# Adding the experts' results into the residual in DRAM by indirect DMAs, instead of on VectorE

## What is computed

```python
x = x + hierarchical_moe(rms_norm(x, g), ...)

def hierarchical_moe(h, ...):            # cut to what matters
    expert, gate = two_best_experts_of_the_best_group(h)      # 2 of 32 for each token
    for e in range(32):                                       # weights: 1024x512, 1024x512, 512x1024
        y_e = (silu(h[tokens of e] @ w_gate[e]) * (h[tokens of e] @ w_up[e])) @ w_down[e]
    return for each token: gate_1 * y_(first expert) + gate_2 * y_(second expert)
```

## Time and profile before

| | us |
|---|---|
| median of three executions | 1812.06 |
| the profiled execution | 1808.48 |
| its span, from the first to the last instruction | 1806.6 |
| TensorE matmuls busy | 1689.5 (94%) |
| VectorE busy | 661.4 (37%) |
| ScalarE busy | 449.3 (25%) |
| GpSimd busy | 170.4 (9%) |

### The profile page before, as it was taken

One profiled execution on the slowest core, in us unless ns is written; L12 is line 12 of the kernel. 1 busy time (PEld: TensorE's weight loads), 2 busy tenths in 40 slices (PEclk: granted clock), 3 DMA queues, 4 the chain that ended last, 5 costly groups with the idle time before them and its releaser, 6 DMA issues.

```text
span 1806.6 us, 21815 instructions
## 1 busy us (share of the span) xinstructions
PE 1689.5 (94%) x8694; PEld 869.9 (48%) x8694; DVE 661.4 (37%) x1266; ACT 449.3 (25%) x807; POOL 170.4 (9%) x172
## 2 busy tenths in 40 slices
PE   7999999799999999999699998999799999999983
PEld 3455454445445555455345558965433333333331
DVE  3279341432122212122468946542522212221223
ACT  2233671233221112111448403332000000000002
POOL 0000000011111111110000013100111111111100
PEclk9999999799999999999899999999799999999997
DMA  9265531399999999999560181054799999999994
GB/s 363 102 238 183 199 129 47 127 397 402 401 401 405 409 403 399 402 413 413 194 246 1 21 128 48 1 208 194 270 396 398 405 408 407 404 420 409 418 417 183
DMA packets 94220, 515.26 MB, mean 285 GB/s; under 512 B 22429, under 2 KB 28157, under 8 KB 69544
## 3 DMA queue, kind: packets, MB, share of 16 engines
q1 hardware_dynamic: 82920, 496.46, 70.7%
q0 software_dynamic: 11200, 17.39, 2.9%
HBM read 506.09 MB, written 27.05 MB: 295 GB/s over the span
## 4 chain that ended last, share of the span: by engine, by line
PE 76%; DMA 13%; DVE 6%; ACT 2%; SPq 2%; issue 1%; DVEq 0%; POOLq 0%
PE bank L863 23%; PE bank L879 11%; PE bank L464 10%; PE bank L456 8%; DMA ring<-in_w_up 6%; DMA ring<-in_w_down 4%; PE bank L850 3%; PE bank L820 3%; PE bank L1232 3%; PE bank L890 2%; PE bank L522 2%; PE bank L687 2%; PE bank L449 1%; DVE arena L2608 1%; PE bank L729 1%
## 5 line engine op out<-in xcount | busy, mean ns | idle before, releaser
L865 PE MATMUL bank<-ring,arena 128*64 128x512 f32 x928 | 421.9, 609 | 0.0
L863 PE MATMUL bank<-ring,arena 128*64 128x512 f32 x752 | 339.4, 605 | 7.3 <-DMA ring<-in_w_up 4.7
L2507 DVE TENSOR_TENSOR arena<-arena,bank 64x512 f32<-64x512 f32 x70 | 48.3, 690 | 561.9 <-ACT arena L1801 561.9
L879 PE MATMUL bank<-ring,arena 128*64 128x512 f32 x544 | 248.0, 598 | 2.3 <-DMA ring<-in_w_down 2.3
L881 PE MATMUL bank<-ring,arena 128*64 128x512 f32 x544 | 247.9, 598 | 0.0
L456 PE MATMUL bank<-arena,ring 128*128 128x512 f32 x560 | 246.3, 596 | 0.0
L863 PEld LDWEIGHTS bank<-ring,arena 128*64 128x64 f32 x752 | 100.7, 139 | 207.0 <-issue 200.9
L863 PE MATMUL bank<-arena 128*64 128x512 f32 x368 | 167.4, 609 | 9.4 <-DMA ring<-in_w_up 5.7
L1801 ACT ACTIVATE arena<-bank 64x512 f32<-64x512 f32 x70 | 41.2, 589 | 512.7 <-PE bank L865 512.7
L1440 POOL DMA_INDIRECT arena<-xnd,smalli x70 | 67.7, 968 | 1058.3 <-PE bank L850 535.9
L456 PEld LDWEIGHTS bank<-arena,ring 128*128 128x128 f32 x560 | 105.8, 191 | 128.1 <-issue 128.1
(11 more groups left out here) (441 smaller groups left out, 1989.7 us busy)
## 6 DMA issues: line engine op xcount, KB each, us to landing
ring<-in_w_down SPq DMA_DIRECT2D x62, 2048.0 KB, 23.2
ring<-in_w_up SPq DMA_DIRECT2D x54, 2048.0 KB, 21.2
ring<-in_w_gate SPq DMA_DIRECT2D x45, 2048.0 KB, 13.4
arena<-in_w_gate SPq DMA_DIRECT2D x19, 2048.0 KB, 25.1
ring<-in_w_mod SPq DMA_DIRECT2D x12, 2048.0 KB, 15.2
ring<-in_w_in SPq DMA_DIRECT2D x10, 2048.0 KB, 17.3
arena<-in_w_up SPq DMA_DIRECT2D x10, 2048.0 KB, 29.3
ring<-in_w_out SPq DMA_DIRECT2D x4, 2048.0 KB, 11.2
```

Of the source, the lines that this page charges most:

```text
L863: pe.matmul(GU[0:CAP, :], x, wg_[:, c, :], start=(c == 0), stop=(c == KD - 1), skip_group_check=True)
L865: mm = pe.matmul(GU[CAP:2 * CAP, :], x, wu_[:, c, :], start=(c == 0), stop=(c == KD - 1), skip_group_check=True)
L879: pe.matmul(Y[0:CAP, :], x, wd_[:, c, 0:512], start=(c == 0), stop=(c == 3), skip_group_check=True)
```

## The change

`yd` and `x2d` are gone. At the start of each stage SyncE stores x_tok in `xd[m]`, 512 rows in DRAM. The scatter adds (`compute_op=ALU.add`) to the rows of `xd[m]`, where a token's first and second expert meet; so each scatter waits until the one before it has landed, and the first one until x_tok is stored. In MoE 0 the share is multiplied by ScalarE on the way out of PSUM. At the end four tile loads bring the sum into x_tok, and VectorE adds nothing. The order on SyncE after MoE 0 is changed: five of the six weights come first, then the tile loads, then the sixth. The tables of rows and tokens are now one, and the shares are made in both stages.

```diff
+            def load_x(m):
+                for q in range(2):
+                    sp.wait_ge(S(f"stored{q}"), 16 * ((BASE[m] + NB[m]) // 2))
+                sp.wait_ge(S("added"), m + 1)
                 for t in range(TT):
+                    sp.dma_start(x_tok[:, t, :], xd[m][P * t:P * t + P, :]).then_inc(S(f"y_in{t}"), 16)
...
                 sp.wait_ge(S("gathered1"), 16 * (BASE[m] // 2 + 1))
+                sp.wait_ge(V.free, V.at(f"outB1{TORDER[-1]}" if m else f"outA1{TT - 1}"))
+                sp.dma_start(xd[m].rearrange("(t p) d -> p t d", p=P), x_tok).then_inc(S("x_out"), 16)
...
             experts(0)
 
-            for q in range(2):
-                sp.wait_ge(S(f"stored{q}"), 16 * (NB[0] // 2))
-            sp.wait_ge(S("yd_done"), 1)
-            load_y(0, yg2)
-            sp.wait_ge(S("x2_ready"), 2)
-            load(U_K)
-            sp.wait_ge(S("x2_ready"), TT)
-            sp.dma_start(x2d.rearrange("(t p) d -> p t d", p=P), x_tok).then_inc(S("x2_out"), 16)
-            for u in range(U_Q, U_DFT + 1):
+            for u in range(U_K, U_DFT):
                 load(u)
+            load_x(0)
+            load(U_DFT)
...
                 def scatter(n):
                     u = n % 2
                     pool.wait_ge(S("y_taken"), n0 + n + 1)
+                    if n:
+                        all_stored(n - 1)
+                    else:
+                        pool.wait_ge(S("x_out"), 16 * (m + 1))
                     pool.indirect_dma_start(
                         out=halves, out_offset=bass.IndirectOffsetOnAxis(ap=homes_any[:, n:n + 1], axis=0),
-                        in_=ys[u], in_offset=None, bounds_check=4 * T - 1, oob_is_err=False)\
+                        in_=ys[u], in_offset=None, bounds_check=2 * T - 1, oob_is_err=False, compute_op=ALU.add)\
                         .then_inc(S(f"stored{u}"), 16)
+
+                def all_stored(n):
+                    pool.wait_ge(S(f"stored{n % 2}"), 16 * ((n0 + n) // 2 + 1))
...
-                    A(ys[q], Y[:, :], ACT.Copy).then_inc(S("y_taken"), 1)
+                    if n == 0:
+                        act.wait_ge(CV.free, CV.at("shares0"))
+                    A(ys[q], Y[:, :], ACT.Copy, scale=share[0][:, n:n + 1]).then_inc(S("y_taken"), 1)
...
-                    act.wait_ge(S("x2_ready"), t + 1)
+                    act.wait_ge(S(f"y_in{t}"), 16 + 16)
                     chain(A(junk, x_tok[:, t, :], ACT.Square, accum_out=ssq[:, t:t + 1]))
...
-                    dve.wait_ge(S(f"y_in{t}"), 16 + 32)
-                    o = x_tok[:, t, :]
-                    chain(STT(o, yg2[t][0], w12[:, t:t + 1], o, ALU.mult, ALU.add))
-                    STT(o, yg2[t][1], w12[:, TT + t:TT + t + 1], o, ALU.mult, ALU.add).then_inc(S("x2_ready"), 1)
...
-                dve.wait_ge(S(f"y_in{t}"), 16 + 64)
-                o = x_tok[:, t, :]
-                chain(TTo(o, o, yg[t][0], ALU.add))
-                TTo(o, o, yg[t][1], ALU.add).then_inc(S("x4_ready"), 1)
```

More of the change, by code:

```diff
@@ L123, in build @@
         xnd = [dram(f"xnd{m}", (T, D)) for m in range(2)]
-        yd = [dram(f"yd{m}", (2 * T, D)) for m in range(2)]
-        x2d = dram("x2d", (T, D))
+        xd = [dram(f"xd{m}", (T, D)) for m in range(2)]
         diag = dram("diag", (2, 16, 8, 16, 16))
@@ L907, in spots @@
                         for r in (0, CAP):
-                            mm = pe.matmul(b[r:r + CAP, 0:NBLK[m] + 1], in_place[:, c, :], at_block[m][:, c, :],
+                            mm = pe.matmul(b[r:r + CAP, 0:NBLK[m]], in_place[:, c, :], share_at[m][:, c, :],
                                            start=(c == 0), stop=(c == 2 * TT - 1), skip_group_check=True)
                     mm.then_inc(CV.full, 1)
[L911 to L917, removed]
                 beside = iter(()) if m else context()
@@ L929, in experts @@
                     if n == 0:
-                        spots()
+                        shares()
                     if n:
@@ L1413, in _ @@
             sp.wait_ge(S("y_taken"), BASE[1] + NB[1])
-            for q in range(2):
-                sp.wait_ge(S(f"stored{q}"), 16 * ((BASE[1] + NB[1]) // 2))
-            sp.wait_ge(S("yd_done"), 2)
-            load_y(1, yg)
+            load_x(1)
             sp.dma_start(fgrow, a["fg"].partition_broadcast(P)).then_inc(S("rows"), 16)
@@ L1459, in experts @@
                     if n == 4:
-                        pool.wait_ge(CV.free, CV.at(f"spots{m}"))
+                        pool.wait_ge(CV.free, CV.at(f"shares{m}"))
                     if n >= 4:
@@ L1490, in experts @@
                 scatter(NB[m] - 1)
-                pool.sem_inc(S("yd_done"), 1)
+                pool.sem_inc(S("added"), 1)
             experts(0)
@@ L2489, in slots, with shares @@
                     b = take(f"slots{m}", CV)
-                    chain(CP(step_[0:CAP], b[0:CAP, 0:nblk]))
-                    chain(TTo(step_[0:CAP], step_[0:CAP], b[0:CAP, 1:nblk + 1], ALU.subtract))
-                    TS(slots_any[:, 2:nblk], step_[0:CAP, 2:nblk], NOWHERE, None, ALU.add).then_inc(CV.free, 1)
-                def spots():
-                    b = take(f"spots{m}", CV)
-                    own(f"slots{m}", CV)
                     chain(CP(step_, b[:, 0:nblk]))
                     chain(TTo(step_, step_, b[:, 1:nblk + 1], ALU.subtract))
-                    TS(homes_any[:, 0:nblk], step_, 2.0, pcol("halfc"), ALU.mult, ALU.add).then_inc(CV.free, 1)
-                    if m:
-                        CP(share[:, 0:nblk], take("shares", CV)[:, 0:nblk]).then_inc(CV.free, 1)
+                    TS(homes_any[:, 0:nblk], step_, 2.0, pcol("halfc"), ALU.mult, ALU.add)
+                    TS(slots_any[:, 2:nblk], step_[0:CAP, 2:nblk], NOWHERE, None, ALU.add).then_inc(CV.free, 1)
+                def shares():
+                    CP(share[m][:, 0:nblk], take(f"shares{m}", CV)[:, 0:nblk]).then_inc(CV.free, 1)
                 def step(n):
```

53 lines of the change are left out of this document (23 added, 30 removed).

## The result

The kernel after takes 1855.0 us, the median of four executions (1853.6 to 1858.8), against 1811.7 us for the kernel before on the same chip (1808.7 to 1815.2). The ratio is 1.024, with a 95% interval from 1.022 to 1.026: 43 us slower. The prediction was 1852.0, 40 us slower. The profiled execution has a span of 1852.7 us, where that of before has 1806.6: 46 us apart and not 43, since the profiled execution of before was 3.2 us under its median and that of after 0.4 us.

The account below looks back on a forecast made before the run. The prediction took both MoE stages as bound by busy DMA engines, with weights landing barely in time or late. Terms 13.8 + 20.1 + 0.3 + 11.3 - 5.6 = +39.9 gave 1852.0 us against the median 1812.06; range 1829 to 1884.

Parts of the forecast that it names:

- MoE 0, +13.8: In MoE 0, some 25 scatters' added fetches (9.8 us) and the store (5.3), less a weight margin of 1.3: +13.8 us.
- The store's part: Storing x to DRAM at the start of MoE 0 pushes later loads back by 5.3 us, less the margin of 1.3.
- MoE 1, +11.3 and +0.3: In MoE 1, fetches of about 35 scatters, 0.32 us each, add 11.3 us; the mostly covered store adds 0.3.
- One by one, 0: In both stages, each scatter's wait for the one before costs nothing while landing stays short enough: 0 us.
- the bound of 12.0: In MoE 1, the landing time in us below which the scatters' waits for one another cost nothing.
- Between the stages, +20.1: After MoE 0, tile loads queue behind five weight loads in one queue, so all that follows is 20.1 us later.
- The end, -5.6: After MoE 1, four tile loads instead of eight start the scaling 6.6 us earlier; with the later landing, -5.6 us.
- the last one lands later by its own fetch: 1.0: At the end, the last scatter lands 1.0 us later (0 to 3), and the serial waits add nothing else.
- A: Rival for the adding scatters: the fetch is free or nearly; +18 us, 1830, up to 1837; chance 0.20.
- B: Rival in MoE 1: the chain of scatters becomes the bound, landing in 14.0 us; 1917 us; chance 0.16.
- C: Rival: not slower, as DMA engines are not full and DMAs in one queue proceed together; -9.6, 1802 us; chance 0.04.

Follow-up runs that it names:

- the first experiment: The kernel after, with SyncE issuing the four tile loads after MoE 0 before the five weights instead of behind them; 1834.0 us, 1.012 of before.
- the best form: The kernel after, with the tile loads ahead of the five weights and the wait ahead of GpSimd's loop moved into its body; 1829.8 us, 1.010 of before.

## Why the prediction was right

The number was helped by luck. The two profiled executions are 46.1 us apart (1808.5 and 1854.6), 6.2 more than the sum of 39.9, from +2.0 between the stages, +4.5 at the end, +1.4 in the mixer and -0.8 each in MoE 0 and ahead of it. The medians show 43.4, since before's profile was a quick one. The mechanisms and three of the four terms held; the term of the end didn't.

*MoE 0, +13.8; measured +13.0.* The step that sized the fetch by the nearest row, the gather, held: the Pool queue's share shows 0.39 us a scatter more, as taken, and taking the adding away gives back 10.6, for 9.8 in the sum. The store's part is only bounded: with fetches gone MoE 0 stays 2.4 above before, and alone it showed 3.8. TensorE's waits began at about 650 us, not 600, and are 10.7 us on w_up, for the 13 to 14 foretold; the rest of the 13.0 is in its longer busy time. The scale on ScalarE's copy, which the text calls free, makes it 0.69 us for 0.60, and no wait of TensorE in MoE 0 comes of it.

*MoE 1, +11.3 and +0.3; measured +11.6.* Here 0.34 us a scatter, for 0.32 taken, and 11.5 are given back without the adding. (35 times 0.32 is 11.2, where the text has 11.3.) The waits for weights grew by 6.2 us and not by 11, from 16.3 to 22.5; TensorE's busy time grew by 3.2.

*One by one, 0; measured 0,* both without adding (0.999 of before) and in the kernel after, whose stages its DMA time explains and whose TensorE never waits for the chain. Landing came to 11.5 (11.9 at most in MoE 1), under the bound of 12.0, and the kernel with two DMAs a block shows what lies behind it. But the margin was luck: the bound comes from the mean pace of 12.8 us, and by the pace of 12.25 at which blocks follow each other when no weight is late it would be 11.45, which a landing of 11.5 has just reached. The scatters did queue up, 22 of them.

*Between the stages, +20.1; measured +22.1.* Right in its mechanism, as the first experiment shows. The square came 32.7 us after the first weight load for 30.4 in the prediction (7.6 + 4 x 5.37 + 1.3). The adding is not what made the difference, since with scatters that write the stretch takes 33.8. At the windows' rates 11.9 MB moved from 889 to 923 us; five weights, one tile and the last scatters' 0.25 MB are 11.3. Parts of the later tiles would be the other 0.6 MB, 1.5 us, and a slower start (349 and 361 GB/s from 893 to 901 us, about 390 behind it) some 0.7; this is worked out and was not tried.

*The end, -5.6; measured -1.1.* This is the step that failed, and within it one term. The part behind the loads' issue was right: from their issue to the end of the span it was 23.8 us (1782.8 to 1806.6) and is 17.4 (1835.3 to 1852.7), -6.4 for -6.6. The term "the last one lands later by its own fetch: 1.0" was the wrong one. From the last take-over to the issue of the loads it was 5.3 us (1777.5 to 1782.8) and is 10.6. The text said that the last scatter but one goes out 4.8 us before the last; it now waits for GpSimd's way through a loop whose bodies are all skipped, which the diff put behind the wait for the last scatter but two. The prediction named what stands behind the moved wait as far as gathers and take-overs go, and left out the 7 us of instructions that lie between two scatters. By the run with the loop freed, the term would have been right otherwise: 5.0 us to the loads and an end of 23.1, for the 23.5 foretold. How much the loop costs hangs on the spacing of the last blocks: with 3 us more of it, in the run that adds in one stage, the end is 24.2.

*The rivals.* A is out, by the queue's share and by the scatters that write. B did not come true at 1917, but it was near: under it the prediction put landing at 14.0, if each fetch waits as often as a write, and it is 11.5, so 3.2 us were added and not 5.7. C is out, by the 23 us that the order of loads in one queue is worth and by the cost of the fetches.

The Trainium skill's rule that an add in the DMA engine has two source reads and so half the rate ("Collectives: The Full Stack", The bandwidth ceiling) is stated there for a ReduceScatter, and the trace of this kernel agrees: a scatter of MoE 0 takes 0.78 us of the engines' time for 0.39. The other rule, that an engine takes turns between queues packet by packet ("DMA: Bandwidth & Descriptors", Queues, rings and completion order), is neither shown nor refuted here, but what the prediction made of it, twice the turns and so 14 us, did not come: a scatter has 144 packets for 80 (a window with two of each shows 288 and 160) and lands 3.2 us later.

## What to carry to other kernels

Adding in the DMA is not free work for an idle engine: it is a read more on each block, so where the DMA engines are full it costs its whole time, and here all that leaving out VectorE's additions gave back in the best form was 8 us at two stage ends, against 26 in the stages. Before a load is moved in a queue, count what stands ahead of it, since five weights of 2.1 MB cost 23 us here, 4.6 each, and two cost 8. And when a wait is put in an engine's program, walk on from it through everything up to the next instruction that someone needs, loops whose bodies are skipped included.

## What the runs showed of the hardware

- An indirect DMA that adds, of up to 128 half rows of 2 KB (0.13 MB of them in the mean in MoE 0, by the queue's bytes, as half the places are empty): issue on GpSimd 1.56 us for 1.00, 144 packets for 80, 0.39 (MoE 0) and 0.34 us (MoE 1) more of the sixteen engines' time while these are full, landing after 11.5 us for 8.3. The bytes that the profile counts do not rise.
- With nothing else on the DMA engines an adding scatter landed after 3.5 and 3.1 us with 0.02 MB (the last two of the kernel after) and after 3.7 and 5.0 us with 0.13 MB (the last of MoE 0, tile loads first, without and with the loop freed). Beside two weight loads that were issued 3 us ahead of it, it took 8.2.
- On GpSimd a loop of 8 passes with two skipped bodies each took 6.6 us (1820.3 to 1826.9 in the kernel after), 0.82 a pass.
- SyncE needed 17.1 us to issue five loads of 2.1 MB in a row (0.4, 0.6, 4.1, 6.6 and 5.2); two took 1.0 us.
- A chain of scatters that wait for one another, each landing after 11.5 us, did not reach TensorE in a stage whose blocks come every 12.25 us with longer steps between (MoE 1 of the kernel after); at 13.1 us and two DMAs a block it did.
